# A two-block network on one core: gate pieces put ahead of the RWKV scan, 64x64 state products, and first products begun before three barriers

## What is computed

```python
h = rms_norm(x, pre_norm_w)
p_rwkv, p_conv, p_pool, p_gate = split(h @ w_in)
y_a = rwkv7_branch(token_shift(p_rwkv))        # 8 heads of 64, a recurrence over 1024 tokens
y_b, y_c = short_conv_branch(p_conv), pool_branch(p_pool)
merged = sum over n of sigmoid(p_gate[n]) * ([y_a, y_b, y_c][n] @ w_branch[n])
x = x + rms_norm(merged @ w_out, post_norm_w)

# one step of the recurrence, per head, state is 64x64:
sa = state @ a_t
state = state * w_t + sa * b_t + v_t * k_t
y_t = state @ r_t
```

## Time and profile before

| | |
|---|---|
| median of 3 runs | 2564.42 us (2559.18 to 2564.59) |
| the profiled execution, its own time | 2563.09 us |
| its span, first to last instruction | 2561.3 us |
| outside the span | 1.8 us |
| mean granted TensorE clock | 0.983 |
| PE / PEld busy | 96% / 76% of the span |
| DVE / ACT / POOL busy | 42% / 30% / 34% |
| DMA | 93 GB/s mean |

### The profile page before, as it was taken

One profiled execution on the slowest core, in us unless ns is written; L12 is line 12 of the kernel. 1 busy time (PEld: TensorE's weight loads), 2 busy tenths in 40 slices (PEclk: granted clock), 3 DMA queues, 4 the chain that ended last, 5 costly groups with the idle time before them and its releaser, 6 DMA issues. The chain is left out here.

```text
span 2561.3 us, 43603 instructions
## 1 busy us (share of the span) xinstructions
PE 2456.7 (96%) x18356; PEld 1958.2 (76%) x18356; DVE 1082.6 (42%) x1328; ACT 777.5 (30%) x1221; POOL 866.0 (34%) x517
## 2 busy tenths in 40 slices
PE   7997999999999999899899999989999999999999
PEld 6775777777768888788777877767768888887887
DVE  5544222222222433554373537743277766760000
ACT  5332222222221111243352115542354343332210
POOL 1333122222101222234362440144246545555622
PEclk9998999999999999999999999999999999999999
DMA  6335223233121221243432330022413232224431
GB/s 203 118 133 174 84 81 85 84 84 84 39 90 33 58 59 55 66 136 124 148 118 83 95 95 28 17 95 67 149 57 99 66 98 82 66 98 148 148 116 66
DMA packets 258581, 238.77 MB, mean 93 GB/s; under 512 B 35888, under 2 KB 218416, under 8 KB 258416
## 3 DMA queue, kind: packets, MB, share of 16 engines
q1 hardware_dynamic: 251536, 224.28, 28.1%
q10 hardware_dynamic: 6880, 12.06, 1.7%
HBM read 166.80 MB, written 61.90 MB: 89 GB/s over the span
## 5 line engine op out<-in xcount | busy, mean ns | idle before, releaser
L177 POOL TENSOR_TENSOR wlo<-wraw,whi 128x1024 fp32r<-128x1024 f32 x87 | 219.2, 2519 | 673.5 <-ACT whi L172 661.7
L3206 PE MATMUL tl_ps_bank<-tl_dn,tl_hid 128*128 128x512 f32 x1056 | 241.2, 391 | 2.5 <-POOL tl_dn L2906 2.5
L3206 PEld LDWEIGHTS tl_ps_bank<-tl_dn,tl_hid 128*128 128x128 f32 x1056 | 199.2, 189 | 44.4 <-issue 2.9
L1041 PE MATMUL rs_ps_bank<-hT_hi,rs_f_hi 128*128 128x512 f32 x384 | 172.2, 448 | 23.7 <-POOL rs_f_lo L805 13.4
L172 ACT CAST whi<-wraw 128x1024 fp32r<-128x1024 f32 x87 | 91.1, 1047 | 310.5 <-PE ring L199 137.0
L199 PE MATMUL br_ps_ps<-hT_hi,whi 128*128 128x512 f32 x448 | 177.9, 397 | 5.8 <-PEq L107 5.8
L199 PE MATMUL br_ps_ps<-hT_lo,whi 128*128 128x512 f32 x448 | 175.6, 392 | 0.0
L199 PE MATMUL br_ps_ps<-hT_hi,wlo 128*128 128x512 f32 x448 | 175.6, 392 | 0.0
L2744 PE MATMUL tl_ps_bank<-tl_M,tl_ophi 128*128 128x512 f32 x528 | 167.0, 390 | 0.0
L1041 PE MATMUL rs_ps_bank<-hT_lo,rs_f_hi 128*128 128x512 f32 x384 | 152.9, 398 | 0.0
L1041 PE MATMUL rs_ps_bank<-hT_hi,rs_f_lo 128*128 128x512 f32 x384 | 152.7, 398 | 0.0
(11 more groups left out here) (449 smaller groups left out, 5544.8 us busy)
## 6 DMA issues: line engine op xcount, KB each, us to landing
wraw<-in_w_in SPq DMA_DIRECT2D x78, 512.0 KB, 4.1
scratch_pg<-rs_f_out SPq DMA_DIRECT2D x48, 256.0 KB, 2.3
wraw<-in_w_out SPq DMA_DIRECT2D x24, 512.0 KB, 3.7
tl_raw<-in_w_gate SPq DMA_DIRECT2D x11, 1024.0 KB, 6.8
tl_raw<-in_w_up SPq DMA_DIRECT2D x11, 1024.0 KB, 5.4
scratch_hid<-tl_H SPq DMA_DIRECT2D x11, 1024.0 KB, 4.9
tl_hidraw<-scratch_hid SPq DMA_DIRECT2D x22, 512.0 KB, 3.3
tl_dnraw<-in_w_down SPq DMA_DIRECT2D x44, 256.0 KB, 2.7
```

The lines of the kernel that those rows point to most:

```text
L177: self.nc.gpsimd.tensor_tensor(self.lo[s][:, :], self.raw[s][:, :], self.hi[s][:, :].bitcast(F32), ALU.subtract).then_inc(self.lo_ready, 1)
L1041: ins = mm(F[:, h, :], a[:, c], b[:, k, cols[h]], start=k == 0 and u == 0, stop=k == KD - 1 and u == 2)
L3206: ins = nc.tensor.matmul(bank[b][:, :], hid[k][:, x, c], dn[n % 2][:, v, :], start=k == 0 and j == 0, stop=k == FF - 1 and j == 2)
```

## The change

The change joins several edits.

1. `phase_rwkv_in` now loads gate tiles 0 and 1 as its `following`, so they sit split in the weight ring at its end. PE computes 5 pieces of gate tile 0 (`READY`) before the barrier, into a PSUM pair `lead` that stays allocated into the scan. The extra load L439 is gone. The last store of the phase (the bonus of head group 3) is no longer waited for at the barrier but at the scan's end.
2. In the scan 11 more pieces stand before the first block (the rest of tile 0, and tile 1 into bank Z), 16 in all. Point 2 of each block (`LEFT`) does nothing, so a block has 22 pieces. The first piece of a tile waits for ACT's copy before its first half and for DVE's before its second.
3. The scan's gate tiles use the weight ring and one more set of buffers; the first two branch tiles are loaded and split in the last block.
4. At the scan's start the order of loads changes: the decay tables, gate tile 2, then a, r and b on SP, constants after them, k and v on ACT's queue. DVE waits for the constants only after its preparation.
5. Q, ST are 64x64 per head; ST is a ring of three; SD and POOL's two operations per block are gone. The carry is 8 matmuls of 64x64 per chunk in two groups of 4, the outputs 16 in two groups of 8. Between matmuls of different rows of the array on one bank PE waits on itself (`gathered`, `carried`, `crossed`).
6. After the last block PE computes 7 of the 8 slices of the first branch tile's first half (21 matmuls) before the barrier.
7. At the end of retention PE computes 18 matmuls of the tail's first two tiles before the barrier, in two banks `lead2`.

```diff
 # phase_rwkv_in
-                    sp.dma_start(d.rbv[:, c, :], bv[:, :]).then_inc(bv_out, 16)
+                    sp.dma_start(d.rbv[:, c, :], bv[:, :]).then_inc(bv_out if c < 3 else d.bonus_kept, 16)
...
-                w.wait_split(sp, N)
-                sp.dma_start(w.raw[1][:, :].rearrange("p (k c) -> p k c", k=KD), merge_source(d, 0, 0)).then_inc(gate_in, 16)
...
                 bonus(3)
+                w.wait_split(pe, N)
+                pe.wait_ge(copied, 2 * N - 2)
+                for k in range(READY):
+                    for h in range(2):
+                        half_products(nc, w, lead[:, h, :], w.slot(N % 2), hT, k, half[h])
 # phase_rwkv_scan, points
-        N, POINTS = TILES * NB, TILES * KD - 1
+        N, POINTS, LEFT = TILES * NB, TILES * KD - 1, 2
+        point = lambda n: n + (n >= LEFT)
...
-            return [t for t in range(1, N) if first <= KD * t - POINTS * i <= last and KD * t > POINTS * i]
+            ends = [(t, KD * (t - 1) - (POINTS - 1) * i) for t in range(2, N)]
+            return [t for t, n in ends if n > 0 and first <= point(n) <= last]
...
+        bank_of = lambda i, x: Z if (i, x) == (0, 1) else F
 # POOL, each block
-                    diagonal(pool, 0)
...
-                    st_sb.wait(pool, i, 1)
-                    diagonal(pool, 1)
 # ACT, start
+                load_swapped(act, 0, "k", d.rk)
+                load_swapped(act, 0, "v", d.rv)
 # DVE
-                dve.wait_ge(consts, 48)
...
+                out(0, 0)
                 dve.wait_ge(loaded, 176)
                 for n in range(3):
                     prepare(0, n)
-                out(0, 0)
+                out(0, 1)
+                dve.wait_ge(consts, 48)
...
-                    for e in range(2):
-                        q_sb.by(nc.vector.tensor_tensor(Q[half[e], :, :, half[e]], narrow(A)[half[e], :, :, :],
-                                                        d.ident[half[e], half[e]].unsqueeze(1).unsqueeze(1).broadcast_to([C, 2, 4, C]), ALU.add))
+                    q_sb.by(nc.vector.tensor_tensor(Q[:, :, :, :], narrow(A),
+                                                    eye[:, :].unsqueeze(1).unsqueeze(1).broadcast_to([P, 2, 4, C]), ALU.add))
 # PE, pieces
-                pieces = iter(range(NB * TILES * KD))
+                pieces = iter(range(READY, NB * TILES * KD))
...
-                    if n == 0:
+                    if n in (0, LEFT):
                         return
...
                     if k == 0:
                         f_lo_ready.wait(pe, i, x + 1)
-                        f_act.wait(pe, i, x)
-                        f_dve.wait(pe, i, x)
+                        if bank is F:
+                            f_act.wait(pe, i, x)
                     c = slice(k * P, (k + 1) * P)
                     for h in range(2):
+                        if h and k == 0 and bank is F:
+                            f_dve.wait(pe, i, x)
...
-                        for n in range(KD):
+                        for n in range(2 * KD - READY):
                             fill(None)
 # PE, state products
+                    gathered.by(ins)
                     fill(21)
-                    q_sb.wait(pe, i, 2)
+                    gathered.wait(pe, i, 1)
+                    q_sb.wait(pe, i, 1)
+
+                    def carry(j, s, e):
+                        for a in range(2):
+                            ins = mm((Z, B)[j][half[e], s, at(a)], Q[half[e], j ^ s, 2 * j + a, :], ST[(2 * i + j) % 3][half[e], nat(a, s), :],
+                                     start=False, stop=a == 1)
+                        return ins
+
+                    def cross(r, e, opens):
+                        for a in range(2):
+                            for j in range(2):
+                                s, first = j ^ r, opens and a == 0 and j == 0
+                                ins = mm(Z[half[e], r, at(2 * s + a)], ST[(2 * i + j) % 3][half[e], nat(a, s), :], rt[half[e], nat(a, s), at(j)],
+                                         start=first, stop=False)
+                        return ins
...
-                        for a in range(2):
-                            for s in range(2):
-                                ins = mm((Z, B)[j][:, s, at(a)], Q[:, j ^ s, 2 * j + a, :], ST[j][:, nat(a, s), :], start=False, stop=a == 1)
-                        st_ps.by(ins)
+                        for e in range(2):
+                            ins = carry(j, 1 - e, e)
+                        carried.by(ins)
...
+                        carried.wait(pe, i, j + 1)
+                        sh.hold(pe)
+                        for e in range(2):
+                            ins = carry(j, e, e)
+                        st_ps.by(ins)
+                        if j:
+                            kept.wait(pe, i, 2)
+                            sh.hold(pe)
+                            for e in range(2):
+                                ins = cross(1 - e, e, True)
+                            crossed.by(ins)
                         fill(22 + j)
+                    crossed.wait(pe, i, 1)
 # PE, scan's end
+                w.wait_split(pe, 2)
+                f_act.wait(pe, NB - 1, TILES)
+                for k in range(KD - 1):
+                    half_products(nc, w, F[:, 0, :], w.slot(2), hT, k, cols[0])
 # phase_retention, PE's end
+                w.wait_split(pe, N)
+                pe.wait_ge(y_lo, NB // 2)
+                for t in range(2):
+                    for k in range(3):
+                        quarter_products(nc, w, lead[t], w.slot(0), t, y, 1, k, half[0])
 # phase_tail
-                        for k in range(4):
+                        for k in range(3 if t < 2 and h == 0 else 0, 4):
```

More of the change, by code:

```diff
@@ L900, in _ @@
                     tok_a.by(nc.scalar.copy(ktok[:, :, :], B[:, 0, :].rearrange("p (h c) -> p h c", c=C)))
+                    if i == 0:
+                        f_product.wait(act, 0, 4)
+                        for x in range(2):
+                            high(act, 1, x)
                     station(i, 1, 3)
@@ L1400, in _, with first_product @@
             def _(pe):
+                def first_product():
+                    w.wait_split(pe, 0)
+                    for h in range(2):
+                        for k in range(KD - 1 if h == 0 else 0, KD):
+                            ins = half_products(nc, w, bank(0, h), w.slot(0), hT, k, half[h])
+                        ins.then_inc(w.product, 1)
                 def product(t):
@@ L2793, in phase_tail @@
         w.phase(sh)
-        bank = [sh.ps(f"bank{n}", [P, HALF]) for n in range(8)]
+        bank = [sh.ps(f"bank{n}", [P, HALF]) for n in range(6)]
+        bank = [lead[0], bank[0], lead[1]] + bank[1:]
         ps, sum_ps = bank[0:4], bank[4:6]
@@ L3301, in program @@
                 rings.close()
-                phase_retention(nc, d, w, Q, hT, over, tab, two(lambda v: two_tiles(d.w_out_2, v, 1)))
-            phase_tail(nc, d, w, hT, base)
+                lead2 = [last.enter_context(nc.psum_tensor(f"lead2_{t}", [P, HALF], F32)) for t in range(2)]
+                phase_retention(nc, d, w, Q, hT, over, tab, lead2, two(lambda v: two_tiles(d.w_out_2, v, 1)))
+            phase_tail(nc, d, w, hT, base, lead2)
 def constants():
```

217 lines of the change are left out of this document (122 added, 95 removed).

## The result

| | before | changed |
|---|---|---|
| median | 2564.51 us (4 runs, 2559.18 to 2565.95) | 2547.09 us (4 runs, 2537.90 to 2550.64) |
| profiled execution | 2563.09 us | 2537.90 us |
| mean granted clock, profiled / the others | 0.983 | 0.987 / 0.981 to 0.982 |

The ratio is 0.9928, 95% interval 0.9901 to 0.9954. The sign was right; the time was not: 2522 (2510 to 2537) was forecast, and the median lies 25 us above it. The profiled execution is the fastest of the four, 16 us above the forecast. I follow that one first.

The account below looks back on a forecast made before the run. The prediction took the length of PE's queue plus its holes to bound these phases. Its terms, 3.5 + 12.8 + 8 + 4 + 7 + 5.4 = 40.7 us, came off 2563.1 to give 2522 us, range 2510 to 2537.

Parts of the forecast that it names:

- The sign: Whole kernel: the change makes it faster; faster by over 0.2% had chance 0.97, within it 0.01, slower 0.02.
- End of the scan: Hole behind the scan: 21 matmuls moved into it, idle about 1 us, clock stays, 7 us gained; no last-block loss forecast.
- Start of the scan: Ahead of the first block: it starts at 229.5 instead of 233.05, 3.5 us gained.
- operands' line: Scan's start: fewer loads ahead of DVE's last operand, all there at 223.3, first block starts at 229.5.
- PE's line: Scan's start: PE goes on at 213.5 after a 1.13 us barrier, eleven pieces take 15.4 us, to 229.0.
- State products: In the 8 blocks: 64x64 products at 0.039 us a record take 3.55 instead of 4.57 us, 8 us in all.
- Pieces taken out: Point 2 of each of 8 blocks left empty: a piece costs 1.60 us there, 12.8 us gained.
- First piece of a tile: Scan's tile starts: PE's 10.3 us of waits for DVE's copy shrink to 4.9, gain 4 us (0 to 6).
- First products ahead of barriers: Scan's end and ahead of the tail: matmuls moved into the holes keep the clock up, gaining 7 and 5.4 us.
- rival C: First products ahead of barriers: what follows was in step with the old time, 12.4 us given back, 2535; chance 0.05.
- D: Scan: fewer pieces make the chip grant the lower clock in part, pieces cost 1.4 us more, 2571; chance 0.02.
- B: Blocks: DVE's X copy 1 us late in each, or gate tile's load delays first block 2.5 us; both 2533; chance 0.12.

Follow-up runs that it names:

- two edits: On the changed kernel, first two branch tiles' loads issued two tiles earlier: 2532.08 us; or ScalarE's two casts of them moved behind its copies in block 7: 2533.89 us.
- experiment 8: Old against new state products on three kernels (changed: 2545.16 against 2547.09, 2541.23 us); its estimate of lower-clock cost is span times one minus mean clock.
- the early loads: Changed kernel with the loads of the first two branch tiles issued two tiles earlier, in block 6: 2532.08 us, ratio 0.9877; run again, 2530.92.
- state_only: Kernel before with only the 64x64 state products of the change: 2560.26 us (12 runs), ratio 0.9989 (0.9980 to 0.9998).

## Why the prediction was wrong

*End of the scan, what I left out* (0 forecast, 12.3 measured; the step that failed first). Edit 3 of the change loads and splits the branch tiles in the last block. I listed it and gave it no term in the sum. I did not ask what is queued behind the wait that it adds to ScalarE's queue: a load issued and its split called for at the same point leave ScalarE waiting for the landing (5.47 and 5.70 us idle), and PE's PM stands behind it. Behind the holes the clock fell (0.67 over the 9.5 us behind the first). This is half of the miss, shown by two edits.

*Start of the scan* (3.5 forecast). The operands' line was right (17.1 forecast, 17.2 measured). PE's line was not: the 1.13 us for "a barrier at which PE itself comes last" left out the 16 increments that PE executes behind the barrier. They were invisible before, inside the hole of 13.37. The time from the projection's end (205.13, and 206.8 in the second profile) to the first transposition fell from 27.5 to 26.9 and 25.3. That is 0.6 to 2.2 us won; most of the difference between the two is the clock, 0.90 in one and 1.00 in the other behind the same hole.

*State products* (8). The size in the blocks was right (1.07 a block for 1.0), the pace of a record too (0.033 to 0.035 for 0.039). The step that failed is the premise of the sum: that in these phases "the time is the length of PE's queue plus its holes", so that a gain in one stretch is a gain of the whole. 2.6 us (0.5 to 5) remained; why, is open.

*Pieces taken out* (12.8): 12.3 in the blocks. Right. *First piece of a tile* (4): idle time fell by 7.0, but 3.1 stood elsewhere in the blocks that did not before (2.8 us "issue", before 0.4, and one more of 0.68 for NV). The sum is right by luck: the last section says what the "issue" stops go with, and that is not this edit.

*First products ahead of barriers* (7.0 and 5.4). The holes and the clock right behind them were as forecast. The sum was not: of 12.4 us 5 to 8 remained. The same step failed as for the state products, a local gain booked as a gain of the whole. That is rival C's outcome in part (all 12.4 given back) and not its mechanism, since the loads did not get late. D did not occur, with a clock of 1.00 over the seven blocks.

In the profiled execution it adds up: 2522.4, with 12.3 for the last block and 2.9 for the start, is 2537.6; it took 2537.9. That is luck in part: this sum books the state products and the first products in full, and the execution is the second fastest of the changed kernel's eight. The median stood 9 us above it, at a clock of 0.982 instead of 0.987 (some 12 us by the estimate of experiment 8). The prediction took a sum made for one profiled execution for the median, since before the two lay 1.3 us apart; but one kernel's executions spread over 10 us, before as after. By the medians, and roughly, the terms that failed are 12 (last block), 1 to 3 (start), 5 (state products) and 4 to 7 (first products): together they cover the 25 us.

The chances: the sign had 0.97 and held. The range's upper end rested on B and C; what happened was neither, and a wait on ScalarE's queue was not among the rivals.

## What to carry to other kernels

When a buffer's owner changes, follow the load that fills it: issue it at least its landing time (4.2 and 4.4 us from issue to cast here) before its consumer's place in the engine's queue, else whatever is queued behind the consumer pays. Count what each engine executes behind a barrier, semaphore increments included, wherever the profile of before hides it in a longer hole. And measure the parts on the whole time: a saving that every pair of profiles shows in its own stretch (8 us here) was worth a third of that. Do not book the fastest execution's profile as the median.

## What the runs showed that I had not expected

A semaphore increment in PE's queue took 0.15 us when PE was idle and next to nothing between running matmuls.

The same hole of 3.35 us was followed by a mean clock of 0.90 in one execution and 1.00 in another (the changed kernel again):

```profile
216.99:232.06 15.07, 15.07 (x67) 12.42 (x67) 4.51 (x4) 4.98 (x7) 5.11 (x3) 1.00 0.96 262
```

PE ran at the lower level in stretches where it was busy all the time: behind the 64 sums of 128x2 of the branches the 20 us from 770 had a mean clock of 0.74 with the early loads, 5 us lost. This is not new: the same stretch lost 3.4 us before (0.83 over the 20 us from 795.4).

And PE stopped in the middle of a group of small matmuls, for 0.4 to 1.8 us, for nothing that the rows name ("issue"). One such stop stood in the scan before (0.39) and none in `state_only`; in nearly every kernel built on the changed one there are two or three, mostly in blocks 1 and 6 (5 with the old state products). In the scans of the 18 profiles there are 34. The packets of the queue `q8 instruction` go with them: each of the 34 stops ended 1.2 to 1.6 us after a packet of 16 KB of that queue had landed (in the changed kernel 277.51 and 277.86 to 278.82, 577.28 and 576.79 to 578.60: landing, then the stop). There are 72 such packets in its scan, and the others go with no stop of this size. So PE waiting for its own code is the likely cause; no run varied it. It would mean that what a change does to the program's length and order moves such stops about.
